# A fused two-block kernel: the down projection's high and low parts split in another order, with three buffers for the middle loop and the last transfers reordered

## What is computed

```python
h = rms_norm(x, norm_ffn[l])
x = x + (jax.nn.silu(h @ w_gate[l]) * (h @ w_up[l])) @ w_down[l]
```

## Time and profile before

| | |
|---|---|
| median of 3 runs | 1577.86 us (1577.79 to 1578.15) |
| the profiled execution's own time | 1577.85 us |
| its span in the profile | 1576.0 us |
| TensorE busy | 1530.5 us, 97% of the span |
| DVE busy | 1061.6 us, 67% |
| ACT busy | 854.3 us, 54% |
| POOL busy | 262.7 us, 17% |
| mean granted clock of TensorE | 0.995 |

### The profile page before, as it was taken

The page is one execution under the profiler, slowest core; times in us unless marked ns, Lnnn a source line. Parts: engine busy times, 40 slices in busy tenths (PEclk is TensorE's granted clock), DMA queues, the critical chain, the costliest instruction groups (busy, mean ns, idle before and its releaser), DMA issues.

```text
span 1576.0 us, 20052 instructions
## 1 busy us (share of the span) xinstructions
PE 1530.5 (97%) x7806; PEld 1238.3 (79%) x7806; DVE 1061.6 (67%) x1717; ACT 854.3 (54%) x1463; POOL 262.7 (17%) x336
## 2 busy tenths in 40 slices
PE   9999999999999999999999999999999999999888
PEld 7877677787887888888877766888778888888766
DVE  4267967866478998999787786675765332345974
ACT  5278776554456888888863434335534332323542
POOL 1000014522234000000172111101201000123110
PEclk9999999999999999999999999999999999999999
DMA  6122121114547999999942111122221332323787
GB/s 236 61 80 81 54 80 55 54 55 159 204 161 233 373 422 420 422 421 421 325 145 101 54 54 54 34 101 66 82 67 55 108 94 94 107 68 125 222 214 193
DMA packets 84849, 250.30 MB, mean 159 GB/s; under 512 B 7536, under 2 KB 10000, under 8 KB 72464
## 3 DMA queue, kind: packets, MB, share of 16 engines
q1 hardware_dynamic: 71456, 216.27, 38.2%
q0 software_dynamic: 6672, 17.85, 4.2%
q10 hardware_dynamic: 6624, 14.88, 2.5%
HBM read 236.39 MB, written 12.60 MB: 158 GB/s over the span
## 4 chain that ended last, share of the span: by engine, by line
PE 76%; DVE 13%; DMA 4%; ACT 3%; issue 1%; POOL 1%; SPq 0%; DVEq 0%; POOLq 0%; ACTq 0%
PE bank L112 70%; PE bank L121 4%; DMA slot<-in_w_down 3%; DVE low L143 2%; PE bank L115 2%; DVE REST L133 1%; DVE REST L143 1%; DVE low L133 1%; DVE REST L146 1%; ACT REST L124 1%; DVE AO L133 1%; ACT REST L127 1%; DVE AL L133 1%; ACT CHH L127 1%; DVE REST L155 1%
## 5 line engine op out<-in xcount | busy, mean ns | idle before, releaser
L133 DVE TENSOR_TENSOR low<-slot,CHH 128x1024 fp32r<-128x1024 f32 (+2 forms) x288 | 312.6, 1126 | 70.4 <-ACT CHH L127 69.5
L127 ACT ACTIVATE CHH<-slot 128x1024 fp32r<-128x1024 f32 (+2 forms) x288 | 269.7, 972 | 115.7 <-PE bank L112 39.9
L143 DVE SCALAR_TENSOR_TENSOR low<-slot,smalls,CHH 128x512 fp32r<-128x512 f32 (+1 forms) x232 | 178.4, 798 | 205.4 <-ACT CHH L127 205.1
L127 ACT ACTIVATE CHH<-slot,smalls 128x512 fp32r<-128x512 f32 (+1 forms) x232 | 156.1, 702 | 172.4 <-PE bank L112 84.6
L112 PE MATMUL bank<-AH,CHH 128*128 128x512 f32 (+1 forms) x640 | 248.5, 388 | 0.2 <-DVE AL L133 0.2
L112 PE MATMUL bank<-AL,CHH 128*128 128x512 f32 (+1 forms) x640 | 242.8, 379 | 0.0
L112 PE MATMUL bank<-AH,low 128*128 128x512 f32 (+1 forms) x640 | 242.5, 379 | 0.0
L112 PE MATMUL bank<-CHH,AH 128*128 128x512 f32 x512 | 215.7, 421 | 3.8 <-DVE low L143 2.8
L112 PE MATMUL bank<-low,AH 128*128 128x512 f32 x512 | 200.9, 392 | 0.0
L112 PE MATMUL bank<-CHH,AL 128*128 128x512 f32 x512 | 200.4, 391 | 0.0
L112 PE MATMUL bank<-CHH,XTF 128*128 128x512 f32 x512 | 161.1, 396 | 1.8 <-DVE REST L130 1.0
(11 more groups left out here) (202 smaller groups left out, 2465.9 us busy)
## 6 DMA issues: line engine op xcount, KB each, us to landing
slot<-in_w_in SPq DMA_DIRECT2D x35, 1024.0 KB, 5.2
slot<-in_w_exp_gate SPq DMA_DIRECT2D x32, 1024.0 KB, 13.3
slot<-in_w_exp_up SPq DMA_DIRECT2D x32, 1024.0 KB, 13.2
slot<-in_w_exp_down SPq DMA_DIRECT2D x32, 1024.0 KB, 13.6
slot<-in_w_gate SPq DMA_DIRECT2D x10, 1024.0 KB, 5.1
slot<-in_w_up SPq DMA_DIRECT2D x10, 1024.0 KB, 5.1
slot<-in_w_out SPq DMA_DIRECT2D x8, 1024.0 KB, 5.9
slot<-in_xkv SPq DMA_DIRECT2D x8, 1024.0 KB, 5.3
```

The source lines that it names most:

```text
L127: return self.e.activation(out, in_, ACT.Copy, scale=scale) if self.e else Issued()
L133: return self.e.tensor_tensor(out, a, b, op) if self.e else Issued()
L143: return self.e.scalar_tensor_tensor(out=out, in0=a, scalar=s, in1=b, op0=op0, op1=op1) if self.e else Issued()
```

## The change

The order in which operands are split and loaded changes, and the memory for high parts. No instruction's size changes but that of cells.

- `CHH` has nine cells, `CHX` is gone, and the high parts of S2 move by 2 KB. The triples use three cells in turn out of nine (0 to 2, 3 to 5, 6 to 8). P3's and P5's units use cells 6, 0, 2 and 4 in turn.
- On ACT the high parts of A12 go behind units 3 to 6, one piece each, and all other operands are spread one piece at a time, in the order of use.
- On DVE `weight_sums` comes one unit earlier: `weight_sums(u - 10)`, so the sums of T(j+2) stand ahead of the low part of Tj. The low parts of token operands follow their high parts by one unit. `first_low` for steps 8 to 10 goes behind units 3 to 5. `add_on` for P2 moves from u = 14 to 16, that for P6 from 25 to 26.
- POOL makes S4 for the last two steps after all of S1 and S2.
- P3's three loads go to the slots of T8, T9 and T10, and P5's to those of T6 and T7 and to P3's first. SP issues P5's first two loads ahead of P3's three.

```diff
+S2_HIGH, S3_HIGH, A22_HIGH = (7, 10, 12, 14), (8, 11, 13, 15), (9, 11, 13, 16)
+S4_HIGH, S1_HIGH = (17, 18, 19, 20), (21, 22, 23, 24)
...
-    CHH = place("CHH", 24, 16, F32R)
+    CHH = place("CHH", 24, 18, F32R)
...
-    HA = [place(f"HA{n}", kb, 11, F32R) for n, kb in enumerate((181, 40, 72, 83, 126))]
-    CHX = place("CHX", 52, 4, F32R)
+    HA = [place(f"HA{n}", kb, 11, F32R) for n, kb in enumerate((181, 42, 72, 83, 126))]
...
-        unit(s, 0, 3, 3 * (j % 2), ("T4", j))
-    pair_cells = itertools.cycle((6, 8, 3, 0))
-    plan_block(1, 512)
-    plan_block(0, 0, add_row=512)
+        unit(s, 0, 3, 3 * (j % 3), ("T4", j))
+    pair_cells = itertools.cycle((6, 0, 2, 4))
+    late = [triples[j].i for j in range(6, FK)]
+    plan_block(1, 512, turns=late[2:])
+    plan_block(0, 0, add_row=512, turns=(*late[:2], late[2]))
     sums_last = [s for s in slots if s.more is not None][FK:]
+    load_order = slots[:-6] + sums_last[:2] + slots[-6:-3] + sums_last[2:]
...
-            if 1 <= u <= 2:
-                for n in (2 * u - 2, 2 * u - 1):
-                    high_of(A12, n, gates_done, ("a", FT - 1))
...
+            if 3 <= u <= 6:
+                high_of(A12, u - 3, gates_done, ("a", FT - 1))
+            for at_units, part, events in ((S2_HIGH, S2, (("S4", FK - 1),)), (S3_HIGH, S3, (gates_done,)),
+                                           (A22_HIGH, A22, (("", "done", D0 + FK - 1),)), (S4_HIGH, S4, (("", "done", D0 + 2 * FK - 1),)),
+                                           (S1_HIGH, S1, (("", "done", D0 + 2 * FK - 1),))):
+                if u in at_units:
+                    high_of(part, at_units.index(u), *events)
...
-            if 11 <= u < 11 + FK:
-                weight_sums(u - 11)
+            if 10 <= u < 10 + FK:
+                weight_sums(u - 10)
             if u >= len(EARLY_UNITS):
                 unit_low(*unit)
...
+            if 3 <= u <= 5:
+                first_low(FK - 6 + u)
+            if 4 <= u <= 7:
+                low_of(A12, u - 4)
+            for at_units, part in ((S2_HIGH, S2), (S3_HIGH, S3), (A22_HIGH, A22), (S4_HIGH, S4), (S1_HIGH, S1)):
+                if u - 1 in at_units:
+                    low_of(part, at_units.index(u - 1))
             if u == 9:
                 add_on("P1", 0, 0)
...
-            if u == 14:
+            if u == 16:
                 add_on("P2", 0, 0, left=True, done=True)
...
-            if u == 25:
+            if u == 26:
                 add_on("P6", 1, 0, bank="P1")
```

More of the change, by code:

```diff
@@ L562, in unit @@
         u = len(units)
-        of = CHX if at == 8 else CHH
-        a = (0 if at == 8 else at) * 512
+        of, a = CHH, at * 512
         chunks = range(len(CH), len(CH) + n)
@@ L576, in _build, with plan_block @@
     pair_cells = itertools.cycle((0, 2, 4, 6))
-    def plan_block(h, n0, add_row=None):
+    def plan_block(h, n0, add_row=None, turns=None):
         for k in range(0, FK, 4):
             m = min(4, FK - k)
-            s = plan_slot(next(in_turn), down_rows[:, h, k:k + m, n0:n0 + 512], m, 512, 3)
+            s = plan_slot(turns[k // 4] if turns else next(in_turn), down_rows[:, h, k:k + m, n0:n0 + 512], m, 512, 3)
             if add_row is not None:
@@ L3170, in vector @@
         for u, unit in enumerate(units):
-            if 11 <= u < 11 + FK:
-                weight_sums(u - 11)
+            if 10 <= u < 10 + FK:
+                weight_sums(u - 10)
             if u >= len(EARLY_UNITS):
                 unit_low(*unit)
[L3175 to L3188, removed]
+            if 3 <= u <= 5:
[5 more added lines that the diff above has]
+                    low_of(part, at_units.index(u - 1))
             if u == 9:
                 add_on("P1", 0, 0)
-            if 10 <= u <= 11:
-                for n in (2 * u - 20, 2 * u - 19):
-                    low_of(A22, n)
-            if u == 14:
+            if u == 16:
                 add_on("P2", 0, 0, left=True, done=True)
[L3196 to L3199, removed]
-            if u == 25:
+            if u == 26:
                 add_on("P6", 1, 0, bank="P1")
@@ L3439, in gpsimd, with fourth_sum @@
             rstd(r4[:, i:i + 1], ss4[:, i:i + 1], 1, 1024.0, ("n4", "sq", i), ("n4", "rs", i))
+        def fourth_sum(k):
+            pool.wait_ge(*at(("S2", k)))
+            pool.tt(parts[:, S4, k, :], parts[:, A12, k, :], parts[:, S2, k, :], ALU.add).then_inc(*mark("pool_down", ("S4", k)))
         for f in range(FT):
@@ L3449, in gpsimd @@
                 pool.tt(parts[:, S2, k, :], parts[:, S1, k, :], parts[:, A11, k, :], ALU.subtract).then_inc(*mark("pool_down", ("S2", k)))
-                pool.wait_ge(*at(("S2", k)))
-                pool.tt(parts[:, S4, k, :], parts[:, A12, k, :], parts[:, S2, k, :], ALU.add).then_inc(*mark("pool_down", ("S4", k)))
+                if f < FT - 2:
+                    fourth_sum(k)
+        fourth_sum(FK - 2)
+        fourth_sum(FK - 1)
         def add_weights(s, to):
@@ L3470, in sync @@
         before = CH[SEG["dq"][0]][0].number
-        for s in slots[:before] + [early] + [x for x in slots[before:] if x is not early]:
+        for s in slots[:before] + [early] + [x for x in load_order[before:] if x is not early]:
             if s.former is not None:
```

## The result

| | before | after |
|---|---|---|
| median | 1577.82 us (6 runs, 1576.37 to 1584.09) | 1594.39 us (6 runs, 1592.84 to 1596.95) |
| ratio to before | | 1.0101, 95% interval 1.0082 to 1.0120 |
| the profiled execution | 1577.85 us, span 1576.0 | 1592.84 us, span 1591.0 |
| mean granted clock | 0.995 | 0.989 |

The change makes the kernel 1% slower. The profiled execution is the shortest of the six, 1.6 us under their median. The sign was forecast, the size was not: 1584.3 was forecast, and 1594.39 lies outside the range of 1576 to 1590.

The account below looks back on a forecast made before the run. TensorE, busy 97% of the span, was taken to wait on DVE's low parts behind the next triple's sums. 1577.85 + 9.4 at P3's start - 3.0 in P5 gave 1584.3 us, range 1576.0 to 1590.0 for 8 in 10.

Parts of the forecast that it names:

- What bounds the kernel: Down projection: TensorE waits for DVE's low parts, held behind the next triple's sums and their landing; 12.0 us idle.
- P1, unit 10 and T0: Start of down projection: no wait in P1, TensorE idles 4.4 us at step 8 of P2, T0 starts at 1486.2.
- the term for half clock: P2, behind the wait of 4.4 us: half clock for 3.4 us, costing 1.7 us.
- 17.3 us for three triples: Middle loop: load and add 10.0, sums and low part 3.1, the triple itself 4.2, where TensorE needs 12.3.
- Three of the signs: Middle loop: DVE waits 3 to 5 us for transfers per three triples, ACT idle for little, triples 5.3 to 6 us apart.
- P3's first load: P3's start: load into T8's slot takes 7.5 us beside P5's adding transfer; P3 starts at 1547.4, 9.4 us lost.
- P5: Late product: early loads remove the wait at step 4, winning 3.0 us; the third add lands in time.
- the rival called slower still: P3 and P5: P5's two early 1024 KB adds hold back P3's loads, TensorE waits inside P3; 1588 to 1594, chance 0.10.
- The faster rival: Down projection: landings come soon enough, TensorE's 12.0 us of waits go; 1566 at best, 1568 to 1573 with few waits; chance 0.13.

Follow-up runs that it names:

- e1: Changed kernel with one line put back, `weight_sums(u - 11)`, so the sums stand one triple ahead: 1581.71 us, ratio 1.0002 to before.
- e2: Kernel before with only the change's line `weight_sums(u - 10)`, sums two triples ahead: 1594.03 us, ratio 1.0092 to before.
- e6: Changed kernel with `weight_sums(u - 9)`, sums three triples ahead: 1628.34 us, ratio 1.0301 to before.
- the fillers: Matmuls that compute nothing, put ahead of TensorE's waits in three runs with sums two ahead: 1595.78, 1592.99 and 1591.26 us.
- e3: Changed kernel with matmuls that compute nothing ahead of step 8 of P2, T5 and T8: 1595.78 us, ratio 1.0097 to before.
- e7: e1 with slots and order of P3's and P5's loads as in the kernel before: 1578.14 us, ratio 0.9988 to before.
- e9: e8 with DVE's sums of T(j+1) behind the low part of Tj instead of ahead: 1572.86 us, ratio 0.9950 to before.
- e8: e7 with the first four stores issued only when P5's last adding transfer has landed: 1572.78 us, ratio 0.9968 to before.
- e12: Changed kernel, old last loads, computing-nothing matmuls ahead of P2's step 8, T0, T3, T6, T7, P2's addition moved: 1591.26 us, ratio 1.0065 to before.

## Why the prediction was wrong, point by point

**What bounds the kernel** was right: the landing ahead of the sums, on an engine that runs in order, decides. e1, e2 and e6 show it apart from the rest of the change.

**P1, unit 10 and T0** came as worked out. No wait stands in P1. DVE was idle 4.72 us ahead of its first sums, and TensorE 3.85 at step 8 of P2 (forecast 4.4). T0 starts 37.1 us behind P1's start, as forecast.

**The step that failed** is the term for half clock. The text had it once, "which costs half of that, 1.7", behind the wait in P2, and then took every triple for 4.2 us in "17.3 us for three triples". T2, T5 and T8 each start behind a wait of 3.9 to 6.0 us, and each of them runs at half clock for part of its time. T2 starts at 1498.33 and T3 at 1505.37, 7.0 us later and not 4.2. Because T(j) ends later, the slot of T(j+5) comes free later, and the lap gets longer by all of it: SP issued T7's load at 1505.56, the adding transfer had landed at 1515.47, 9.9 us later (forecast 10.0), and T5 started at 1518.62, 3.15 us after that (forecast 3.1). By the table the first lap, T2 to T5, took 20.3 us (forecast 17.3), and 3.0 of half clock explain the 3.0. The second took 19.8 (2.5 over): 1.4 of half clock and 0.9 because T10's load and adding transfer, with POOL's issue between, took 10.9 us from issue to landing instead of 10.0. T8 to P3 took 16.0 (1.9 over, 1.7 of half clock). P3 took 16.7 instead of 15.0, again 1.7. With 0.7 us up to T2, where P2 lost 3.0 to half clock and not 1.7, the excess is 9.8, and the last matmul is 9.7 later than forecast. Half clock in all is some 10.7 us where the sum had 1.7. The size of that term accounts for 9.0 of the 9.7 by the windows, and for 7.8 to 8.5 by the laps, where not all of P2's loss reaches T2; the fillers gave back up to 5.3 of it by P3 and left 4 to 5 in place.

It was a choice from one pair of rows: the clock fell behind 2.89 us of idle time and not behind 2.84. I carried the worse case to the first wait and to no other, though the forecast itself had three more, of 3.6 to 3.7 us.

**Three of the signs failed too.** DVE waited 5.6 to 7.4 us per three triples for transfers, where 3 to 5 were given, and ACT, which was to be idle for little, was idle 33.5 us in eight waits between 1485 and 1544, the longest (6.99 us) for sums of weights made by DVE. The three triples came 19.8 to 20.3 us apart, 6.7 each, where 5.3 to 6 were given.

**P3's first load** took 7.5 us from SP's issue at 1544.45 to ACT's start at 1551.94, as estimated. Its wait is 1.82 us, forecast 1.8. **P5** has no wait, as forecast, and its third add landed 7.5 us after its issue and in time. **The sum** against the profiled execution: 1577.85, less 1.1 for P1's earlier start, and 16.1 for the longer down projection, is 1592.8.

**The range** was too narrow at its upper end for the same reason. It allowed for longer transfers but not for half clock at each wait. At its lower end the terms named add up to some 1575 and not to 1576 (1584.3 less 4.8 for three laps, 3 for P3's load and 1.7), which changes nothing here. The measured time lies just above the upper edge of the rival called slower still, but not by its mechanism: in the changed kernel nothing waits inside P3. In e1, where the middle loop is quick, that mechanism does show, at P3's start, and in e3 too (a wait of 5.76 us).

**The faster rival**, with short transfers, did not come. Adding transfers of 256 KB took 4.1 to 7.7 us in the changed kernel. The Trainium skill ("DMA: Bandwidth & Descriptors", "Anatomy of one DMA — SWDGE (gpsimd) path") gives about 2.0 us and the bytes over 436 GB/s, an estimated 2.6 us for that size, and no run here comes near it: the shortest took 3.6 us (e3).

**What the order of use is worth.** With the sums one ahead (e7), T0 starts 2.4 us sooner than in the kernel before. That gain was in the change, and the sums' place covered it. In the whole time it is not clear of the noise (ratio 0.9988, 0.9972 to 1.0004). What the third buffer alone is worth was not tried.

## What to carry to other kernels

Ahead of work that another engine waits for, put nothing on an in-order engine that itself waits for a transfer; and when such a wait is moved one item ahead, count how many items the chain of slot, load, add and use now spans, because its length is divided by that number. If TensorE then idles for some 4 to 6 us again and again, as here, charge half clock behind each wait, and inside the loop, since a later end frees the slot later. A load moved ahead of another can hold it back (P3's first load took 13.1 us in e1): see what it delays before counting what it saves.

## What the runs showed of the hardware that was not expected

- The length of an idle time does not tell whether half clock follows. Behind 2.84 us the clock stayed at 1.00 in the kernel before, behind 2.89 it fell. In the changed kernel it fell to 0.50 at 1555.6, 1.2 us after the restart from an idle time of only 1.82 us, and in e9 it did not fall behind 1.86 us. In e3 waits of 2.20 and 2.67 us had none behind them, in e8 one of 2.31 us had. From P1 to the last matmul, stretches at half clock lasted 3.4 or 6.8 us of the record, part of it idle, and one of 10.2 us stands at each of five waits of 7.7 to 9.4 us in e6.
- Adding transfers of 1024 KB took 9.6 to 16.4 us in all these runs, and a plain load of the same size about 5.0 us with none of them beside it and 13.1 us beside two of them (e1).
- Work that nobody needs, put ahead of five starts, made the middle loop 5.3 us shorter (e12, one profile), though at two of them it held TensorE back.
